# Sample attention in the convolution stage: keys transposed by VectorE, scores in halves of one bank, four passes of two batches

## What is computed

```python
proj = a @ w_in;  q, k, v, hc, gb, gc = split(proj)         # 3 x 512 for attention, 3 x 512 for the convolution
att  = dilated_attention(q, k, v, rel_bias)                 # prompt; sample below
u    = gc * hc;  y_conv = gb * conv3(u)
h    = h + concat(rms_norm(att), rms_norm(y_conv)) @ w_out
h    = h + experts(rms_norm(h));  h = h + (p @ w_proj) * sigmoid(rms_norm(h) @ w_ple)

def dilated_attention_sample(q, k_all, v_all, rel_bias):    # q: (8, 4, 8 heads, 64)
    # keys of three patterns: (128, step 1), (512, step 4), (2048, step 16), over 2048 cached rows and 4 new ones
    s = einsum('bthc,btkhc->bthk', q, kg) * 64**-0.5 + bias
    p = softmax(where(valid, s, NEG))
    return einsum('bthk,btkhc->bthc', p, vg)
```

## Time and profile before

| | us |
|---|---|
| median of three runs | 1085.08 (1082.19 to 1086.80) |
| the profiled execution, its own time | 1086.79 |
| its span in the profile | 1085.0 |
| PE busy | 1039.2 |
| VectorE (DVE) busy | 522.5 |
| ScalarE (ACT) busy | 309.7 |
| GpSimd (POOL) busy | 239.5 |
| the convolution stage without its first four steps | 291.4 to 502.0 |

### The profile page before, as it was taken

One profiled execution on the slowest core, in us unless ns is written; L12 is line 12 of the kernel. 1 busy time (PEld: TensorE's weight loads), 2 busy tenths in 40 slices (PEclk: granted clock), 3 DMA queues, 4 the chain that ended last, 5 costly groups with the idle time before them and its releaser, 6 DMA issues.

```text
span 1085.0 us, 15705 instructions
## 1 busy us (share of the span) xinstructions
PE 1039.2 (96%) x5834; PEld 621.3 (57%) x5834; DVE 522.5 (48%) x1175; ACT 309.7 (29%) x657; POOL 239.5 (22%) x272
## 2 busy tenths in 40 slices
PE   6999999899999999999999999989999998989997
PEld 5888875555778777766555554334433333335443
DVE  6836635788743464555566564341111110047674
ACT  2332323677433422301111123111111111244431
POOL 0100001144833462441022112222131110130000
PEclk9999999899999999999999998999999998989999
DMA  9713214930554656762874237999999999874321
GB/s 316 187 32 115 74 50 122 299 85 9 214 180 141 214 181 213 237 235 78 340 273 145 97 116 268 394 365 417 418 409 408 420 420 397 336 289 156 122 78 77
DMA packets 99261, 242.12 MB, mean 223 GB/s; under 512 B 21206, under 2 KB 56958, under 8 KB 84528
## 3 DMA queue, kind: packets, MB, share of 16 engines
q1 hardware_dynamic: 88544, 212.10, 53.9%
q0 software_dynamic: 9920, 26.38, 6.4%
q10 hardware_dynamic: 720, 2.62, 0.6%
HBM read 210.12 MB, written 35.65 MB: 227 GB/s over the span
## 4 chain that ended last, share of the span: by engine, by line
PE 88%; DVE 4%; DMA 4%; ACT 1%; issue 1%; POOL 1%; SPq 0%; DVEq 0%; POOLq 0%; ACTq 0%
PE pair L2914 14%; PE pair L2596 13%; PE pair L3117 13%; PE pair L2969 10%; PE pair L3221 7%; PE pair L3139 6%; PE pair L3216 3%; PE pair L2737 2%; DMA R<-in_w_up 2%; PE pair L2752 2%; PE pair L2711 2%; PE pair L3040 2%; PE pair L3104 1%; PE pair L2813 1%; PE pair L2830 1%; PE pair L2817 1%
## 5 line engine op out<-in xcount | busy, mean ns | idle before, releaser
L2914 PE MATMUL pair<-R 128*128 128x264 f32 x672 | 161.9, 392 | 0.1
L3117 PE MATMUL pair<-R 128*32 128x512 f32 (+2 forms) x896 | 153.1, 610 | 5.9 <-DMA R<-in_w_up 3.6
L2596 PE MATMUL pair<-R 128*128 128x256 f32 x672 | 149.6, 381 | 1.8 <-DVE R L1756 1.8
L2596 PEld LDWEIGHTS pair<-R 128*128 128x128 f32 x672 | 126.9, 191 | 20.2 <-DVE R L1756 2.2
L2914 PEld LDWEIGHTS pair<-R 128*128 128x128 f32 x672 | 124.6, 192 | 23.7 <-issue 3.5
L2969 PE MATMUL pair<-R 128*128 128x512 f32 x256 | 114.9, 599 | 0.0
L2327 DVE TENSOR_TENSOR R<-pair,R 128x256 f32<-128x256 f32 x21 | 8.9, 425 | 209.1 <-ACT R L1517 209.1
L3117 PEld LDWEIGHTS pair<-R 128*32 128x32 f32 (+2 forms) x896 | 48.6, 126 | 94.7 <-issue 90.2
L3139 PE MATMUL pair<-R,bias 128*32 128x512 f32 (+2 forms) x448 | 76.3, 596 | 2.7 <-issue 2.1
L2969 PEld LDWEIGHTS pair<-R 128*128 128x128 f32 x256 | 47.1, 190 | 52.2 <-issue 51.5
L3221 PE MATMUL pair<-R 128*128 128x512 f32 x168 | 73.0, 593 | 0.0
(11 more groups left out here) (368 smaller groups left out, 1535.7 us busy)
## 6 DMA issues: line engine op xcount, KB each, us to landing
R<-in_w_gate SPq DMA_DIRECT2D x32, 1024.0 KB, 13.0
R<-in_w_up SPq DMA_DIRECT2D x32, 1024.0 KB, 16.4
R<-in_w_down SPq DMA_DIRECT2D x32, 1024.0 KB, 17.3
R<-in_w_in SPq DMA_DIRECT2D x12, 1024.0 KB, 8.5
R<-in_x_prompt SPq DMA_DIRECT2D x16, 512.0 KB, 3.9
R<-in_cache_k SPq DMA_DIRECT2D x8, 1024.0 KB, 5.0
R<-in_cache_v SPq DMA_DIRECT2D x8, 1024.0 KB, 5.0
R<-y_dram SPq DMA_DIRECT2D x16, 512.0 KB, 5.2
```

The source lines that it names most:

```text
L2596: last = mm(qbank(p, part, k), lhs[:, c, :], rhs[:, c, :], start=(c == 0), stop=(c == 3))
L2914: last = mm(cbank(n, k), lhs[:, c, :], rhs[:, c, :], start=(c == 0), stop=(c == 3))
L3117: last = mm(bk[2 + u][r, :].rearrange("p (w f) -> p w f", w=2), xgT[u][:, c, r], wgu[s][:, :, c, :], start=(c == 0), stop=(c == DC - 1))
```

## The change

Keys are loaded in another layout, so that a block of 32 partitions holds one head pair. VectorE's transposes of 32 by 32 blocks then put 32 head dimensions of each of the four pairs on the partitions, and no transposes on PE and no copies on ScalarE are left. A key item becomes 16 DMAs: for each head pair one of 256 KB (32 partitions, 16 pieces of 512 bytes in each) and three of 64 KB. The value items keep 4 DMAs with rows in the matching order. Scores of two batches share one bank: strips 0 and 1 of partitions hold the near scores of the even and odd heads, strips 2 and 3 the far and new ones; each is summed over two halves of the head dimension. There are four passes of two batches, in two alternating banks; after the bias the maxima and denominators of upper and lower half are combined by small copies. The parts list is made by `sample_order`, the order of the items changes, and the transposes of the sample tokens' q and k are replaced by products of 32x32 pieces.

```diff
-ITEMS = [("k", b) for b in range(5)] + [("v", 0), ("k", 5), ("v", 1), ("k", 6), ("v", 2), ("k", 7)] + [("v", b) for b in range(3, NB)]
+ITEMS = [("k", 0), ("k", 1), ("k", 2), ("v", 0), ("k", 3), ("v", 1), ("k", 4), ("v", 2),
+         ("k", 5), ("v", 3), ("k", 6), ("v", 4), ("k", 7), ("v", 5), ("v", 6), ("v", 7)]
+ARRIVES = {"k": 16 * NG * (1 + FARC), "v": 16 * (1 + FARC)}
...
-SAMPLE_PARTS = (("key", 0, 0), ("key", 0, 1), ("key", 0, 2), ("key", 0, 3), ("score", 0),
...
+def sample_order():
+
+    parts = []
+    for g in range(NPASS + 1):
+        keys = [[("key", 2 * g + d, gg) for gg in range(NG)] if g < NPASS else [] for d in range(2)]
+        if g == 0:
+            parts += keys[0] + [("score", 0)] + keys[1] + [("score", 1), ("soft", 0)]
+            continue
+        b = 2 * g - 2
+        parts += [*keys[0][0:1], ("norm", g - 1), *keys[0][1:2], ("turn", g - 1), *keys[0][2:4]]
+        if g < NPASS:
+            parts += [("score", 2 * g)]
+        parts += [("weigh", b), *keys[1][0:2], ("sum", b), ("weigh", b + 1), *keys[1][2:4]]
+        if g < NPASS:
+            parts += [("score", 2 * g + 1), ("soft", g)]
+        parts += [("sum", b + 1)]
+    return parts
...
-ROOM = {"key": 4, "score": 4, "turn": 6, "weigh": 8, "sum": 4}
+ROOM = {"key": 4, "score": 6, "soft": 2, "norm": 2, "turn": 4, "weigh": 8, "sum": 4}
...
# SP, load_item
+            if kind == "k":
+                for pair in range(NG):
+                    rows, heads = slice(32 * pair, 32 * pair + 32), slice(P * pair, P * pair + P)
+                    sp.dma_start(kv[rows, 0:4, :].rearrange("p j (r x) -> p (j r) x", r=4),
+                                 ck[b][PAST - NEAR:PAST, heads].rearrange("(p m) x -> p m x", m=16)).then_inc(arrived, 16)
+                    for k in range(FARC):
+                        sp.dma_start(kv[rows, 4 + k, :].rearrange("p (t x) -> p t x", t=NT),
+                                     ck[b][512 * k:512 * k + 512, heads].rearrange("(p a) x -> p a x", a=16)[:, 0:NT, :]).then_inc(arrived, 16)
+                return
...
# ScalarE
-        def keep_near(b, gg):
...
-        def keep_far(b, gg):
...
         def exp_sample(g):
             act.wait_ge(S("ss_scored"), g + 1)
-            act.activation(Es, Es, ACT.Exp, bias=nms, scale=-1.0, accum_out=dens).then_inc(S("ss_exp"), 1)
+            for rows, n in ((slice(0, 64), NEAR), (slice(64, P), FAR + SAMP)):
+                act.activation(Es[rows, 0:n], Es[rows, 0:n], ACT.Exp, bias=nms[rows, :], scale=-1.0,
+                               accum_out=dens[rows, :]).then_inc(S("ss_exp"), 1)
...
# VectorE
+        def turn_keys(b, gg):
+            slot, arrived = item("k", b)
+            kv = KV[slot]
+            if gg == 0:
+                dve.wait_ge(S(f"ring_in{slot}"), arrived)
+                if b >= 1:
+                    dve.wait_ge(S("ss_done"), b)
+                else:
+                    dve.wait_ge(S("ssa_full"), 1)
+            part = slice(32 * gg, 32 * gg + 32)
+            dve.transpose(near[:, gg, :].rearrange("p (r j y) -> p j r y", r=4, j=4),
+                          kv[:, 0:4, :].rearrange("p j (r x) -> p j r x", r=4)[:, :, :, part])
+            dve.transpose(far[:, gg, :].rearrange("p (k t y) -> p k t y", k=FARC, t=NT),
+                          kv[:, 4:7, :].rearrange("p k (t x) -> p k t x", t=NT)[:, :, :, part]).then_inc(S("kt_done"), 1)
...
         def score_sample(g):
...
+            scores = bk[6 + g % 2]
+            for rows, n in ((slice(0, 64), NEAR), (slice(64, P), FAR + SAMP)):
+                last = dve.tensor_tensor_reduce(Es[rows, 0:n], scores[rows, 0:n], bias_s[rows, 0:n], -1.0, 3e38, ALU.add, ALU.min, nms[rows, :])
+            then(last)
+            then(dve.tensor_copy(other_nms[0:64, :], nms[64:P, :]))
+            then(dve.tensor_tensor(nms[0:64, :], nms[0:64, :], other_nms[0:64, :], ALU.min))
+            dve.tensor_copy(nms[64:P, :], nms[0:64, :]).then_inc(S("ss_scored"), 1)
...
# PE, sample tokens' q and k
+                    for i in range(NG):
+                        at = AD * part + P * i + 32 * g
+                        last = mm(dst[32 * i:32 * i + 32, P * g:P * g + n], qks[0:n, at:at + 32], ident[0:n, 0:n], start=True, stop=True)
...
# PE
-        def keys(b, gg):
...
         def score_keys(b):
+            g, second = divmod(b, 2)
+            out = bk[6 + g % 2]
+            pe.wait_ge(S("kt_done"), NG * b + NG)
...
+            for half in range(2):
+                for c0, c1, far_row, rhs in ((0, NEAR, 0, near), (0, FAR, 1, far), (FAR, FAR + SAMP, 1, kts)):
+                    for hh in range(2):
+                        last = mm(out[strips[2 * far_row + hh], c0:c1], qbd[g % 2][:, second, 2 * hh + half, :], rhs[:, 2 * hh + half, :],
+                                  start=(second == 0 and half == 0 and c0 == 0), stop=(second == 1 and half == 1 and c1 != FAR))
             last.then_inc(S("ss_done"), 1)
```

More of the change, by code:

```diff
@@ L207 @@
-ROOM = {"key": 4, "score": 4, "turn": 6, "weigh": 8, "sum": 4}
+    return i % 3, sum(ARRIVES[k] for k, _ in ITEMS[i % 3:i + 1:3])
+RING_USED = tuple(sum(ARRIVES[k] for k, _ in ITEMS[s::3]) for s in range(3))
+def sample_order():
[14 more added lines that the diff above has]
+    return parts
@@ L224, with place_of @@
 PARTS_AT = spread_parts()
-def place_of(kind, b, gg=None):
-    return next(s for s, parts in PARTS_AT.items() for part in parts if part[0:2] == (kind, b) and (gg is None or part[2] == gg))
+def place_of(part):
+    return next(s for s, parts in PARTS_AT.items() if part in parts)
 NSTAT = 6
@@ L602, in _build @@
     ssc, rc = small[:, 88:97], small[:, 97:106]
-    nms, dens, rdens = small[:, 106:107], small[:, 107:108], small[:, 108:109]
+    nms, dens, rdens, other_nms, other_dens = (small[:, 106 + k:107 + k] for k in range(5))
     ssa, ra = small[:, 140:149], small[:, 150:159]
@@ L1412, in sample_part @@
+            last.then_inc(S("st_done"), 1)
         def sample_part(kind, b, *more):
-            if kind == "key":
-                keep_near(b, more[0])
-                keep_far(b, more[0])
-            elif kind == "turn":
+            if kind == "soft":
+                exp_sample(b)
+            if kind == "turn":
                 keep_ps(b)
-            if "soft" in more:
-                exp_sample(b // 4)
         act.wait_ge(S("ot_full"), NGROUP)
@@ L2094, in sample_part @@
         def sample_part(kind, b, *more):
-            if "norm" in more:
-                normalise_sample(0 if kind == "key" else 1)
+            if kind == "key":
+                turn_keys(b, more[0])
+            if kind == "soft":
+                score_sample(b)
+            if kind == "norm":
+                normalise_sample(b)
             if kind == "weigh":
                 mask_sample(b)
-            if "soft" in more:
-                score_sample(b // 4)
-            if kind == "score" and b == 3:
-                spread_q(1)
-                new_bias(1)
             if kind == "sum":
                 keep_sum(b)
-            if "sum" in more:
-                keep_sum(more[-1])
         dve.wait_ge(S("late_in"), 16 * NLATE)
@@ L2881, in sample_part @@
         def sample_part(kind, *more):
-            if kind == "key":
-                keys(more[0], more[1])
             if kind == "score":
@@ L2889, in sample_part @@
                 weigh_values(more[0])
[L2890 to L2891 removed]
+            if kind == "sum":
+                sum_values(more[0])
         def conv_product(n, k):
```

251 lines of the change are left out of this document (104 added, 147 removed).

## The result

The changed kernel takes **1191.84 us** (median of four runs, 1182.98 to 1196.78), the kernel before 1085.39 in the same comparison (1082.19 to 1086.80): 1.0963 times as long, with an interval of 1.0907 to 1.1018. That is 107 us more than the forecast of 1085 and far outside its range.

What follows compares the result with a forecast made beforehand. TensorE, 96% busy, was taken as the bound. Terms: -24.6 transposes, +13.1 weight waits, +8.6 VectorE waits, +1.1 sample turns, +1.8 clock = 0.0, so 1085 us; own case 1078 to 1093, full range 1069 to 1104.

Steps and rivals of the forecast that it cites:

- part 3: SP's load queue in the convolution stage: slower key issues make conv weights late, +13.1 us; value items hide.
- The key transposes left TensorE: Convolution stage: key transposes, 0.44 and 0.33 us a head pair, leave TensorE, -24.6 us.
- Block 1 started: Convolution stage: block 1 starts at 298.5, lasts 16.3 us, and TensorE reaches block 2 at 314.8.
- The waits of scores and turns: Convolution stage: TensorE's scores and probability turns wait for VectorE, +8.6 us, between 3 and 15.
- The products that turn the sample's q and k: Attention stage: 32 small products replace 8 transposes, +1.1 us, ends 0.5 and 3.
- The clock: TensorE's products run at a lower clock: +1.8 us in the forecast sum.
- A: Convolution stage: loads keep up, with key issues of 0.42 us and smaller waits; 1070 us, chance 0.25.
- B: Convolution stage: SP becomes the bound at 0.65 us an issue, 10.4 an item; 1098 us, chance 0.17.
- C: VectorE's transposes run at half rate, 2.2 us a head pair; 1102 us, chance 0.09.
- D: Near and far scores don't overlap on TensorE, 0.7 us more in each half; 1096 us, chance 0.04.
- E: A key item's DMAs run one by one, 34 us an item; 1170 us, chance 0.03.
- the weighed rule on transfers under 64 KB: Key loads: small transfers are descriptor-dominated, estimated at 17 us an item and some +50 us in all.

Runs made afterwards that it cites:

- v_natural: Changed kernel with the value loads' patterns of before, so the sample output weighs rows in another order: 1110.5 us in one run.
- weights_first: Changed kernel with value loads of before, VectorE transposes writing with a step of four, and key items issued later, behind conv weights: 1104.00 us, ratio 1.0155.
- old_k_new_form: Kernel before with only the change's 16 DMAs per key item, so its scores are others: 1097.33 us in one run.
- row_read: Changed kernel with value loads of before, whole-block VectorE transposes, and row order mended in the scaling of the probabilities: 1118.96 us, ratio 1.0321.
- turn_later: row_read with key items issued later, scores one part later and all but the last turn of probabilities one key turn later: 1087.86 us, ratio 1.0023.
- old_v_new_form: Kernel before with only the change's value load patterns, so the output has another row order: 1188.4 us in one run.
- v_by_strip: Changed kernel with each value item cut into 8 DMAs of 32 partitions, keeping the change's row order: 1128.21 us, ratio 1.0393.

## Why the prediction was wrong

**The step that failed** is in part 3: "the value items, still 4 DMAs, hide". It put the value loads at no cost. I counted DMAs and bytes and did not read the shape of their patterns, though the changed kernel's lines L791 to L794 show it (`j p (r d)` with j = 4). Priced alone in the old kernel the pattern costs 104 us; in the changed kernel it costs 81 of the 107.
The other steps:

1. The key transposes left TensorE, as its order of instructions had shown; VectorE's rows L2092 and L2094 stand in their place.
2. Block 1 started at 298.62, forecast 298.5 (which is two products behind 294.96, not the three that the text says), and TensorE stood at block 2 at 316.15, forecast 314.8. The lengths of the later blocks were not measured alone.
3. Issues were right in size: a head pair's four DMAs take 2.24 us (one starts at 302.20, the next at 304.44), an item 8.9, where I had 8.3; block 2's weights went out at 309.85, forecast 307.5. The waits were undersized even without the value pattern: 20.3 us in six waits in `v_natural`, forecast 13.1 in four; block 2's was 6.1 in the changed kernel, forecast 3.7. The old kernel with the new key loads had only 7.9 in three. A size that was short is the load: I had 6.0 us from issue to landing, `v_natural` has 6.0 as its fastest and 8.6 as its median. `weights_first` shows that the mechanism was the right one.
4. The price of VectorE's transposes was right: 700 and 534 ns, forecast 0.69 and 0.56. The waits of scores and turns were twice what I had: 11.2 + 5.6 = 16.8 us in `v_natural`, forecast 8.6, outside my bounds of 3 to 15.
5. The products that turn the sample's q and k cost nothing to be seen: the first product behind the squares starts at 290.85, before at 291.25.
6. The clock was undersized: 166.5 us for the 672 product records in `v_natural`, 161.9 before, so +4.6 where I had +1.8 (within its bounds), and +14.5 in the changed kernel.

By the measured terms `v_natural` comes to -24.6 + 20.3 + 16.8 + 4.6 = +17.1 against a span that is 23.4 longer; some 6 us have no row of their own. So even without the failed step the forecast was 25 us too low, outside its range of 1069 to 1104: the waits for weights came half again as large as I had put them, and those for VectorE twice as large.

The rivals: A (1070) had the waits for weights going away. They do in `weights_first`, but its time stays above before, because VectorE's waits take their place. B had the right side and the right engine, SP, but not the reason: a key issue took 0.56 us, at its point of 0.55 and short of its 0.65, and the large loss came from SP being held by the value loads, which B did not have. C is excluded by 700 ns a transpose (1.23 us a head pair, where the estimate from the Trainium skill, VectorE: DVE Perf Modes, "The three transpose paths", had 2.2: the count by elements held, the one by squares did not), D by the scores of a batch, 2.15 us from their start to the next product (364.98 to 367.13), against 1.70 in the chain of before and 0.20 lost behind it. E is excluded by 182 GB/s over 300 to 310, with keys alone in flight: 1.8 MB in the 34 us of that rival would be some 54 GB/s. The estimate of +50 us from the weighed rule on transfers under 64 KB did not come: the key loads by themselves cost 13 us in `old_k_new_form`.

Open: the roughly 12 us of the stage and 6 us of `v_natural` without a row, and why `v_natural` (one run, 1110.5) lies 8 us below `row_read`, which differs from it in the scaling and the buffer that the turn reads. Open too is what exactly holds SP. It is not peculiar to the value loads (the eight loads of `w_out` hold it for 19.74 us in the kernel before), and no run changed the number of loads outstanding alone.

## What to carry to other kernels

Read a load's patterns, not its count and bytes: when a rearrangement moves a dimension of 4 to the outside of a DRAM pattern, price the load as one on a quarter of the engines, and then look at what is queued behind it on the same issuing engine. If rows must come in such an order, put the partitions outermost and mend the order where it is cheap. And when work is moved off the bounding engine, set what it gives back against all the new waits together: here 24.6 us of transposes left TensorE, and after the orders of loads and parts had been improved, the waits left (19.7 us in `turn_later`) still took most of that.

## What the runs showed of the hardware

- Loads whose DRAM pattern has 4 as its slowest dimension: DMA share 0.23 at 61 GB/s (changed kernel) and 0.24 at 56 GB/s (`old_v_new_form`) with nothing else flowing, and mostly 9 to 17 us for SP to issue three of 256 KB, against 1.9 for the same bytes with 128 outermost.
- Loads that hold up SP delay loads that have nothing to do with them: a conv weight load took 15.00 us to issue behind a value item in `old_v_new_form`; the median of these loads in the kernel before is 0.61.
- Value loads cut to 32 partitions keep far more than four engines in use, at more engine time for the bytes: a share of 0.91 at 175 GB/s over the stage in `v_by_strip`, 0.78 at 190 in `v_natural`. Key loads in pieces of 512 bytes show 1.22 at 182 GB/s over 300 to 310, the experts' loads 0.96 at 382.
- VectorE's transpose in blocks of 32 of 128x512 fp32 elements takes 700 ns with whole blocks, and 1093 ns when it writes with a step of four elements; a scaling of 64x384 that writes so takes 894 ns, one of 64x512 672 ns; why the smaller one is slower is not known.
